# Sixteen first-stage tiles loaded during the query stage, and eight more tokens by gathered rows

## The reference, cut to what matters

```python
def peer_ffn(h, w_q, sub_keys, u_tab, v_tab):
    q = (xc @ w_q).reshape(t, PEER_HEADS, 2, PEER_QDIM // 2)
    sc = jnp.einsum('thpc,hpnc->thpn', q, sub_keys).astype(jnp.float32)
    v_half, i_half = lax.top_k(sc, PEER_TOPK_HALF)
    ...
    top_s, pos = lax.top_k(cand, PEER_TOPK)
    expert = jnp.take_along_axis(cand_idx, pos, axis=-1)
    g = jax.nn.softmax(top_s, axis=-1)
    u = u_tab[expert]
    act = jax.nn.gelu(jnp.einsum('thkd,td->thk', u, xc).astype(jnp.float32), approximate=False)
    w = (g * act).astype(xc.dtype)
    return jnp.einsum('thk,thkd->td', w, v_tab[expert])
```

## Time and profile before

| | us |
|---|---|
| median of 3 runs | 1919.02 |
| lowest, highest | 1915.56, 1919.78 |
| the profiled execution, its own time | 1924.92 |
| the span from its first to its last instruction | 1923.1 |

### The profile page before, as it was taken

How to read it: one execution, slowest core, us unless ns; L and a number is a source line. 1 busy time by engine, 2 the same in 40 slices (tenths; PEclk the granted TensorE clock), 3 DMA queues, 4 the chain that set the end, 5 groups by cost and what they waited for, 6 DMA issues and landing times.

```text
span 1923.1 us, 35495 instructions
## 1 busy us (share of the span) xinstructions
PE 1868.3 (97%) x13794; PEld 1770.8 (92%) x13794; DVE 1358.0 (71%) x2860; ACT 485.3 (25%) x898; POOL 456.2 (24%) x412
## 2 busy tenths in 40 slices
PE   8999999999999899999999999999999999999998
PEld 7888888878999899999999998899989999999998
DVE  6899886785898776667744347779987676775442
ACT  6557644565411100000000046552110000000001
POOL 0000000000135443333333200002455333333330
PEclk9999999999999999999999999999999999999999
DMA  6554324534599999999999953258999999999994
GB/s 262 211 194 174 122 95 154 173 100 146 170 409 409 409 408 397 392 397 394 388 403 410 379 173 121 89 164 318 408 409 408 409 398 390 395 392 393 409 410 189
DMA packets 148007, 580.19 MB, mean 302 GB/s; under 512 B 13596, under 2 KB 13724, under 8 KB 145216
## 3 DMA queue, kind: packets, MB, share of 16 engines
q1 hardware_dynamic: 91712, 376.37, 52.1%
q0 software_dynamic: 56192, 202.47, 26.7%
HBM read 576.62 MB, written 1.05 MB: 300 GB/s over the span
## 4 chain that ended last, share of the span: by engine, by line
PE 67%; DMA 12%; DVE 6%; ACT 2%; issue 1%; POOL 0%; SPq 0%; DVEq 0%; ACTq 0%; POOLq 0%
PE bank L2645 25%; PE bank L2609 22%; DMA wbuf<-in_peer_u 5%; PE bank L373 5%; PE bank L375 5%; PE bank L374 5%; DMA wbuf<-in_peer_v 4%; DMA e_gbuf<-in_peer_rows,e_row_few 3%; PE bank L2501 2%; DVE tile_lo L282 1%; PE bank L2570 1%; ACT tile_hi L274 0%; PE bank L1617 0%; PE bank L2657 0%; DVE proj L1058 0%
## 5 line engine op out<-in xcount | busy, mean ns | idle before, releaser
L2609 PE MATMUL bank<-h_dense,wbuf 128*128 128x160 f32 x4096 | 576.6, 301 | 12.1 <-DMA wbuf<-in_peer_u 10.6
L2609 PEld LDWEIGHTS bank<-h_dense,wbuf 128*128 128x128 f32 x4096 | 560.2, 190 | 19.6 <-issue 12.9
L2645 PE MATMUL bank<-e_hidden,wbuf 128*128 (+1 forms) x4096 | 571.8, 300 | 2.2 <-DMA wbuf<-in_peer_v 1.7
L2645 PEld LDWEIGHTS bank<-e_hidden,wbuf 128*128 128x128 f32 x4096 | 558.3, 190 | 6.5 <-issue 6.2
L274 ACT ACTIVATE tile_hi<-wbuf 128x1024 fp32r<-128x1024 f32 (+2 forms) x117 | 121.8, 1047 | 364.3 <-PE bank L2645 289.9
L2445 POOL DMA_INDIRECT e_gbuf<-in_peer_rows,e_row_at x128 | 141.5, 1106 | 275.1 <-PE bank L2609 157.3
L2445 POOL DMA_INDIRECT e_gbuf<-in_peer_v,e_row_at x128 | 143.4, 1120 | 253.6 <-PE bank L2645 191.7
L282 DVE TENSOR_TENSOR tile_lo<-wbuf,tile_hi 128x1024 fp32r<-128x1024 f32 (+2 forms) x117 | 140.3, 1211 | 87.6 <-ACT tile_hi L274 86.9
L2466 DVE SCALAR_TENSOR_TENSOR x_tok<-e_gbuf,e_acts,x_tok 128x1024 f32<-128x1024 f32 x128 | 164.1, 1282 | 38.3 <-DMA e_gbuf<-in_peer_v,e_row_at 31.6
L2734 ACT ACTIVATE e_hidden<-bank 128x320 f32<-128x320 f32 x128 | 56.0, 437 | 529.3 <-PE bank L2609 529.2
L384 PE MATMUL bank<-a_parts,tile_hi 128*128 128x512 f32 x512 | 181.0, 399 | 0.0
(11 more groups left out here) (404 smaller groups left out, 2552.5 us busy)
## 6 DMA issues: line engine op xcount, KB each, us to landing
wbuf<-in_peer_u SPq DMA_DIRECT2D x128, 1024.0 KB
wbuf<-in_peer_v SPq DMA_DIRECT2D x128, 1024.0 KB
wbuf<-in_w_in SPq DMA_DIRECT2D x16, 2048.0 KB, 7.4
wbuf<-in_peer_q SPq DMA_DIRECT2D x32, 512.0 KB
wbuf<-in_hyb_in SPq DMA_DIRECT2D x16, 512.0 KB
wbuf<-in_mla_uq SPq DMA_DIRECT2D x9, 512.0 KB
wbuf<-in_mla_in SPq DMA_DIRECT2D x8, 528.0 KB
wbuf<-in_w_v SPq DMA_DIRECT2D x2, 2048.0 KB, 7.2
```

The costliest lines, as they stand in the source:

```text
L2609: last = nc.tensor.matmul(bank[:, j // 2 % 2, j % 2 * S:j % 2 * S + DENSE], deep[:, slot, k * P:(k + 1) * P], h_dense[:, k, :], start=(k = ...
L2645: last = nc.tensor.matmul(turned_x(g, k)[:, 0:DENSE], deep[:, slot, k * P:(k + 1) * P], hidden[:, bass.ds(a, 1), 0:DENSE].rearrange("p a t ...
```

## The change

`DENSE` falls from 160 to 152. Tokens 152 to 159 (`RARES = 8`) are looked up too, sixteen picks of each per item, so 8 items more for `u` and 8 more for `v`: 104 + 104 = 208 items. Their row numbers, their token vectors and their shares are brought into a layout of 16 blocks of 8 partitions, each by 16 small DMAs from GpSimd's queue (`row_rare`, `x_rare`, `share_rare`).

The first 16 tiles of `u` no longer pass through the ring. SP loads them between the loads of the query tiles and just ahead of the first ring pairs, into memory that is free by then: eight tiles into the eight `gbuf` buffers, four into `stage`, four into the third ring buffer (`wbuf[:, 2]`). The ring starts with tile 16. In return GpSimd's items 0 to 7 wait for the tile in their buffer to be used. `row_gain` moves from `gbuf` to `x_few`.

```diff
-DENSE = S - GATHERED - FEWS
-HIDDEN = 192
+RARES = 8
+DENSE = S - GATHERED - FEWS - RARES
+HIDDEN = DENSE
+EARLY_TILES = 16
...
-    DOTS = SHARED + FEWS
+    DOTS = SHARED + FEWS + RARES
     ITEMS = 2 * DOTS
...
+    RARE_BLOCK = [(slice(RARES * n, RARES * n + RARES), slice(RARES * n, RARES * n + RARES)) for n in range(P // RARES)]
+    X_RARE_AT = EARLY + 12
...
+    early = ([gbuf[:, 2 * n:2 * n + 2, :] for n in range(GBUFS // 2)] + [whole_tiles(56), whole_tiles(24)]
+             + [g["wbuf"][:, 2, :].rearrange("p (j c) -> p j c", c=TILE)[:, 2 * n:2 * n + 2, 0:D] for n in range(2)])
...
+    def load_early(sp, n):
+        sp.dma_start(early[n], U[2 * n:2 * n + 2, :, :].rearrange("a p c -> p a c")).then_inc(early_loaded[n // 2], DMA)
...
-            load_pair(sp, 2 * p, p)
-        with sp.Fori(1, ROUNDS) as r:
+            if p == SLOTS // 2:
+                load_early(sp, 6)
+            elif p > SLOTS // 2:
+                load_early(sp, 7)
+            load_pair(sp, EARLY_TILES + 2 * p, p)
+        with sp.Fori(EARLY_ROUNDS + 1, ROUNDS) as r:
...
         for j in range(STEP, HALVES):
             load_tile(sp, g, ins, M_Q + j)
+            if j < STEP + 5:
+                load_early(sp, j - STEP)
+            if j == STEP + 5:
+                sp.wait_ge(rows_ready, 3)
+                sp.wait_ge(xn_turned, 4)
+                load_early(sp, 5)
...
             if n == EARLY:
                 pool.wait_ge(rows_ready, 8)
                 for rows, picks in FEW_BLOCK:
                     pool.dma_start(row_few[rows, :], row_of_few[FEW, picks]).then_inc(moved, DMA)
-                pool.wait_ge(moved, 2 * MOVED)
+                for rows, picks in RARE_BLOCK:
+                    pool.dma_start(row_rare[rows, :], row_of_few[RARE, picks]).then_inc(moved, DMA)
+                pool.wait_ge(moved, ROWS_MOVED)
+            if n == X_RARE_AT:
+                pool.wait_ge(used, M_U + EARLY_TILES)
+                for rows, picks in RARE_BLOCK:
+                    pool.dma_start(x_rare[rows, :], x_scaled[RARE, :]).then_inc(moved, DMA)
             if n == SHARES_AT:
+                pool.wait_ge(moved, X_RARE_MOVED)
                 pool.wait_ge(soft_step, 5)
...
+                for rows, picks in RARE_BLOCK:
+                    pool.dma_start(share_rare[rows, :], pick[RARE, 1, 2, picks]).then_inc(moved, DMA)
             if n >= EARLY:
                 pool.wait_ge(used, M_U + pace(n))
+            if n < GBUFS:
+                pool.wait_ge(used, M_U + n + 1)
...
+        for j in range(EARLY_TILES):
+            if j % 4 == 0:
+                pe.wait_ge(early_loaded[j // 4], 2 * DMA * (i + 1))
+            if j % 2 == 0:
+                pe.wait_ge(bank_free, j // 2 + 1)
+            all_rows(early[j // 2][:, j % 2, :], j)
+        with pe.Fori(0, (TURN_AT - EARLY_TILES) // STEP) as r:
             for j in range(STEP):
-                experts(r, STEP, 0, j)
+                experts(r, STEP, EARLY_TILES, j)
...
-                for t, start, size, at in ((1, P + GATHERED, GATHERED, 0), (0, DENSE, FEWS, GATHERED)):
-                    nc.tensor.matmul(turned_x(g, k)[:, start:start + size], x[:, t, k * P:(k + 1) * P],
+                for total, start, size, at in ((x[:, 1, :], P + GATHERED, GATHERED, 0), (x[:, 0, :], P + FEW.start, FEWS, GATHERED),
+                                               (sum_rare, DENSE, RARES, GATHERED + FEWS)):
+                    nc.tensor.matmul(turned_x(g, k)[:, start:start + size], total[:, k * P:(k + 1) * P],
                                      const(g, "fold")[:, at:at + size], start=False, stop=False, skip_group_check=True)
...
+        nc.vector.memset(sum_rare, 0.0).then_inc(picks_kept, 1)
```

More of the change, by code:

```diff
@@ L95 @@
 CST, _n = {}, 0
[L96 removed]
+for _name, _width in (("ident", P), ("causal", SC), ("freq64", 32), ("freq32", 16), ("iota", NKEYS), ("fold", GATHERED + FEWS + RARES)):
     CST[_name] = _n
@@ L2312, in expert_layer @@
     junk = flat(48, 56).rearrange("p (t d) -> p t d", t=NT)
-    x_few, x_scaled = g["x_few"], junk[FEW, 1, :]
+    x_few, x_rare, sum_rare = g["x_few"], g["x_rare"], g["sum_rare"]
+    x_scaled = junk[LOW, 1, :]
     JUNK_OVER = 48 * S // HIDDEN // 2
@@ L2417, in gpsimd @@
         for rows, picks in FEW_BLOCK:
-            pool.dma_start(x_few[rows, :], x_scaled).then_inc(moved, DMA)
-        pool.wait_ge(moved, MOVED)
+            pool.dma_start(x_few[rows, :], x_scaled[FEW, :]).then_inc(moved, DMA)
+        pool.wait_ge(moved, X_FEW_MOVED)
         pool.wait_ge(rows_ready, 5)
@@ L2437, in gpsimd @@
                 table, rows = U_ROWS, row_few[:, n - EARLY:n - EARLY + 1]
+            elif DOTS - RARES <= n < DOTS:
+                table, rows = U_ROWS, row_rare[:, n - DOTS + RARES:n - DOTS + RARES + 1]
             elif n < DOTS:
@@ L2600, in tensor, with all_rows @@
         pe.wait_ge(sc_kept[1], 5)
+        def all_rows(tile, j):
+            for k in range(KT):
+                last = nc.tensor.matmul(bank[:, j // 2 % 2, j % 2 * S:j % 2 * S + DENSE], tile[:, k * P:(k + 1) * P],
+                                        h_dense[:, k, :], start=(k == 0), stop=(k == KT - 1))
+            last.then_inc(used, 1)
         def experts(q, width, base, j):
@@ L2605, in experts @@
             if j % 2 == 0:
-                pe.wait_ge(ring_loaded[slot // 2], DMA * (width // STEP * q + pairs_loaded(slot // 2) + (base + j) // STEP + 1))
+                pe.wait_ge(ring_loaded[slot // 2],
+                           DMA * (width // STEP * q + pairs_loaded(slot // 2) + (base + j) // STEP - EARLY_ROUNDS + 1))
                 pe.wait_ge(bank_free, width // 2 * q + (base + j) // 2 + 1)
-            for k in range(KT):
-                last = nc.tensor.matmul(bank[:, j // 2 % 2, j % 2 * S:j % 2 * S + DENSE], deep[:, slot, k * P:(k + 1) * P],
-                                        h_dense[:, k, :], start=(k == 0), stop=(k == KT - 1))
-            last.then_inc(used, 1)
-        with pe.Fori(0, TURN_AT // STEP) as r:
+            all_rows(deep[:, slot, :], j)
+        for j in range(EARLY_TILES):
[5 more added lines that the diff above has]
+        with pe.Fori(0, (TURN_AT - EARLY_TILES) // STEP) as r:
             for j in range(STEP):
-                experts(r, STEP, 0, j)
+                experts(r, STEP, EARLY_TILES, j)
         pe.wait_ge(soft_step, 4 * NT)
```

73 lines of the change are left out of this document (48 added, 25 removed).

## The result

The changed kernel takes 1970.33 us (median of 4 runs, 1961.94 to 1972.81) against 1918.49 us (1915.56 to 1919.78) for the kernel before beside it: a ratio of 1.0259 with a 95% interval of 1.0233 to 1.0286, so 52 us slower. The forecast was 1921 (1903 to 1941), and it missed by 49 us.

What follows compares the result with a forecast made beforehand. DMA, near 409 GB/s, was taken as the bound: 522.2 + 541 of transfers + 20 idle gives tile 241 at 1083, against 1084.8 before. With small terms, +1 us a layer, +2 in all: 1921 us (1903 to 1941).

Steps and rivals of the forecast that it cites:

- TensorE gets less: Expert layers: 8 columns fewer make a matmul 262 ns, 13 ns less, 27 us a layer (20 to 28).
- DMA now idles at the start: Start of the first stage: about 28 units move from 522.2 to 578, leaving DMA 20 us idle (16 to 25).
- The query stage: Ahead of the first expert layer: the early loads among the query tiles cost 0.5 us (0 to 2).
- Second stage at 405 or more: Up to tile 241: DMA at 405 GB/s or more, also in the second stage, where it was 397.
- Waits: TensorE: 25 to 35 us in total for the picks, some 10 to 20 us a layer for tiles.
- The fold: Layer's end: `add_folded` has 24 matmuls in place of 16, so the fold takes 5.2 us instead of 3.5.
- Tile 241 within 5 us of 561 us after the first tile: Second stage: a check on when TensorE reaches tile 241, counted from the layer's first tile.
- `x_rare` stops GpSimd for 16 x 0.52 = 8 us, which the eight buffers cover: First stage, GpSimd's queue: issuing 16 vector copies takes 8 us, hidden by the eight gather buffers.
- the copies of `share_rare` ... 0.5 (0 to 4): While VectorE makes one-hot rows: these copies hold GpSimd another 8 us, costing 0.5 us a layer (0 to 4).
- rival B: First stage: small copies in the gathers' queue starve VectorE and idle DMA, +18 us, 1937 us; chance 0.22.
- 217 tiles + 203 items = 420 units again, + 1 ... + 1 because a pair has to be whole: Up to tile 241: DMA moves 422 units a layer, 541 us at 409 GB/s.
- rival C: Second stage's end: items trail the tiles and fill DMA's last us, 6 us a layer faster, 1909 us; chance 0.14.

Runs made afterwards that it cites:

- the version with all mends: Changed kernel with `x_rare` copies issued by SP, early and ring pairs used in turn, and items spread up to tile 245: 1951.92 us, ratio 1.0179 to 1.0181 not distinguished.

## Why the prediction was wrong, by its own steps

**What held.** *TensorE gets less*: 262 ns a matmul, to the digit. *DMA now idles at the start*: 20 us counted, 5.8 + 9.1 + 5.4 = 20.3 found up to 580; item 16 at 575 against "about 572". In part this is luck. The parts that the prediction lists up to 578 add up to 26 units, not to its 28; the trace has 30 up to 580, but 3.6 of them are loads that should have been there already (below). *The query stage*: from its first load to the first tile it takes 74.7 us, 74.8 before, so not even the 0.5 us came. *Second stage at 405 or more*: 409 and 410 but for 382 from 840 to 870. There GpSimd stood 14.08 us for a free buffer, and VectorE, which frees them, 15.56 us for the first group of weights of the second half. *Waits*: 36.1 us for the picks, just above 25 to 35, and 19.5 us a layer for pairs (10 to 20). *The fold*: 5.26 us against 5.2. And the frame: DMA bounds the layer; with TensorE's gain put back (160 columns) the time moves by 4.5 us (10.6 in the layers), not by 54.

**Its own signs of being wrong.** "Tile 241 within 5 us of 561 us after the first tile": the last item is issued 582.5 us after it. "B is right if DMA falls under 400 at 590 to 680": it has 336 from 600 to 620.

**What failed, first: "`x_rare` stops GpSimd for 16 x 0.52 = 8 us, which the eight buffers cover".** The stop was 8.24 us, as counted. The buffers did not cover it. They cover a stop only with gathers that have landed, and there were none: VectorE waited 0.41 and 2.12 us for items 26 and 27, which were issued ahead of the copies, so all eight were under way. The rows of before had said so: VectorE waited for such rows 17 times there, and the second dot of the earlier trace rows shows one of the waits. The 8.6 us from issue to landing is the median over all stages; items 26 to 30 took 16 to 18 us now and 17 to 19 before. So the stop went through to VectorE nearly whole. The dot of item 27 starts 1.4 us later than before (611.3 against 610.0), that of item 28 11.8 us later (624.3 against 612.5), and the one ahead of the picks 9.7 us later (661.7 against 652.0). GpSimd's further 8.91 us without a semaphore to wait for end about when the last copy can have landed; the trace doesn't say what holds it, and VectorE loses nothing more by it: item 31 behind it lands in 9.8 us.

The cost in DMA's time: 3.6 us in the slow stretch behind the copies, 600 to 620. Then TensorE stood 18 us for the picks, and DMA lost 5.5 us in 667 to 700, where the kernel without any copies has 407 GB/s: the item at 688.38 waited 7.21 us for TensorE's tiles there. The kernel without the `x_rare` copies alone still has the `share_rare` copies in that stretch and 394 GB/s, a loss of 1.2 us, so "the copies of `share_rare` ... 0.5 (0 to 4)" holds, and most of the 5.5 is a result of the late picks. Counted up to the last item of layer 0, DMA is idle for 31.3 us in the changed kernel and for 20.5 without copies. That is 11 us a layer for the copies in place of 0.5, and the two layers are 10.3 and 9.2 us longer by them.

This is rival B, which had 0.22. It named the mechanism (buffers that don't cover the stops, the last item of the few tokens at 665 or later; its dot starts at 667.8), its place (590 to 680, under 400 GB/s) and its sign, but priced it at 18 us and sat on a forecast that was too low by the next term. The argument against it, "DMA is not full at that point any more", holds for the `row_rare` copies, issued at 562 with DMA at 299 GB/s, and item 16 is out at 575. It does not hold for those of `x_rare`: DMA was at 408 from 580 on.

The Trainium skill has about 2.0 us fixed for a DMA issued by GpSimd, plus its bytes (DMA: Bandwidth & Descriptors, on the anatomy of one DMA). The rows here differ: 12.9 us for 32 KB. The measurement decides.

**Second: "217 tiles + 203 items = 420 units again, + 1 ... + 1 because a pair has to be whole".** At the last item DMA had moved 430 units, not 422, which is 10 us of each layer. The packets of the trace say whose they are: 223.3 of SP's queue, where the step has 218, and 205.9 of GpSimd's, where it has 204; 0.8 are loads of instructions.

- 3.6 of SP's units are the tail of the loads ahead of the stage. SP issues nothing between 516 and 558 us, and yet moves 3.6 units after 521.2; the last two of these loads land 4.0 and 6.5 us after the first tile. "The ring holds tiles 16 to 23 when the stage begins" was not so, and "16 tiles are moved ahead" was 16 less these. In layer 1 it is 5.4 units.
- 1.7 are work ahead in the ring. The step has one unit of it if DMA is the bound, where it had 6 in the kernel before. The trace has SP 3.5 tiles ahead of TensorE at the last item now, and 4.8 before, so the lead hardly changes. The chain shows why: a pair takes 14 us from issue to landing, against 2.56 us for its bytes alone, and SP issues one about every 4.6 us, so three or four pairs of the ring are under way at once and each is partly moved while TensorE waits for the first. The work ahead is not gone, it is spread over pairs that are of no use yet.
- 1.9 are gathers and small copies beyond the 203 items and `x_rare`.

The items' price itself was right up to the last item. Against the kernel with 152 columns and 16 items less, the one without copies moves 15.7 units more there (429.0 and 413.3), 20 us, and has its last item 21.5 us later, counted from the first tile. Behind the last item it takes 5.6 us longer, and with that two layers cost 52 us for 32 items, 1.6 us an item where 1.28 was counted. The end is where TensorE works off what it holds: the last wait for a pair ends at 1113.0, DMA has 147 GB/s from 1120 on, and TensorE needs 30 us more. The prediction had 36.7 us and 0 to 3 behind the last item, and the trace has 39.5; 1.7 us of it are a lower clock (last section).

The sum again, per layer and against the forecast's 0 for it, with what was measured: (430 - 422) x 1.28 = 10, 31 - 20 = 11, tail 1: 22 us, and the layer was 23 us longer.

**Two slips in the prediction's rows.** The dot at 652.0 that the earlier trace rows gives to item 47 is that of item 43, the one the picks wait for; item 47's starts at 663.6. So gathers came one in 2.6 us, not in 2.3, and the 55% of rival C are 49%. And 1921 with -8 and +12 is 1913 to 1933, not 1911 to 1933. Neither moves the forecast.

**What stays open.** Why GpSimd stands 8.91 us, and what makes the rate fall behind the copies: their full surroundings alone, or also their form (rows of 8 partitions each); the version with all mends has both in SP's queue too. Why the three mends don't add up is read from one wait and not tested. The Trainium skill has a rule that bears on the form: a DMA is spread over the largest number of engines, up to 16, that divides the slowest dimension of both its patterns, with an exception for some copies issued by GpSimd (DMA: Bandwidth & Descriptors, on why a DMA increments its semaphore by 16). By either, an estimate, a copy of 8 partitions would put its data on 8 engines. No run here shows which engines the packets took; the mean busy share of all 16 was 1.04 at 336 GB/s, but gathers and ring pairs ran on them at the same time.

## What to carry to other kernels

When two engines lie within a few us of each other, work moved from one to the other has to be priced at the ceiling of the second, and so does every us in which the second idles: here 54 us of TensorE's time bought 16 units a layer that DMA had no room for. Buffers cover a stop of the queue that fills them only with what has landed: if the consumer waits a little for each landing, all of them are under way, and the stop comes through (8.2 us of issues, 10.4 us at VectorE here). So look at the consumer's waits, and at the time to landing in that stretch, not at its median. And an early load pays by itself (5 to 7 us here, 13 with its order and pace set to match) as long as its gain isn't spent on new transfers.
